# Weight splits, first chunk and last squares at the borders of three MLPs

## What is computed

```
def first_block(x, ...):
    h = x
    for layer in range(2):
        if layer == 0:
            h = h + gla_mixer(rms_norm(h, a_norm), ...)
        else:
            k_sh, v_sh = shared_kv(h, kv_norm, w_kv, k_norm)
            h = h + diff_mixer(rms_norm(h, b_norm), k_sh, v_sh, ...)
        h = h + sqrelu_mlp(rms_norm(h, mlp_norm[layer]), mlp_w1[layer], mlp_w2[layer])
    return h

def second_block(x, mem, ...):
    u = rms_norm_2(h, norm_mix)
    proj = u @ w_in
    ...
    h = h + merged @ w_mix_out
    h = h + memory_cross_attention(...)
    u = rms_norm_2(h, norm_mlp)
    h = h + jnp.square(jax.nn.relu(u @ w_mlp_up)) @ w_mlp_down
    return h
```

## Time and profile before

| | us |
|---|---|
| median of 3 runs | 1561.04 |
| fastest, slowest | 1559.62, 1563.72 |
| the profiled execution | 1560.55 |
| its span | 1558.6 |
| PE busy | 1421.5 (91%) |
| DVE busy | 1034.0 (66%) |
| ACT busy | 894.4 (57%) |
| POOL busy | 334.9 (21%) |

### The profile page before, as it was taken

One profiled execution on the slowest core, in us unless ns is written; L12 is line 12 of the kernel. 1 busy time (PEld: TensorE's weight loads), 2 busy tenths in 40 slices (PEclk: granted clock), 3 DMA queues, 4 the chain that ended last, 5 costly groups with the idle time before them and its releaser, 6 DMA issues. The chain is left out here.

```text
span 1558.6 us, 29975 instructions
## 1 busy us (share of the span) xinstructions
PE 1421.5 (91%) x11466; PEld 1289.0 (83%) x11466; DVE 1034.0 (66%) x1638; ACT 894.4 (57%) x1705; POOL 334.9 (21%) x337
## 2 busy tenths in 40 slices
PE   7998999999889999999887799898898889799999
PEld 6888899988668999989776677778777679599998
DVE  6787666566656666667999755567576666375555
ACT  4455555456556555558988645454565466365543
POOL 2002211150004111138877000004000003051111
PEclk9999999999978999999999899999999989999999
DMA  7323455545713555535344322325334335055552
GB/s 306 126 106 122 147 200 194 189 163 118 207 55 121 204 190 188 193 132 189 136 144 153 108 86 105 108 102 180 122 129 156 126 124 180 32 193 199 193 189 82
DMA packets 35603, 233.72 MB, mean 150 GB/s; under 512 B 4000, under 2 KB 7072, under 8 KB 8352
## 3 DMA queue, kind: packets, MB, share of 16 engines
q1 hardware_dynamic: 31104, 223.75, 40.4%
q10 hardware_dynamic: 3216, 4.19, 1.7%
q0 software_dynamic: 1168, 4.20, 0.9%
HBM read 227.93 MB, written 4.19 MB: 149 GB/s over the span
## 5 line engine op out<-in xcount | busy, mean ns | idle before, releaser
L1593 DVE TENSOR_TENSOR w_lo<-raw,w_hi 128x1024 bf16<-128x1024 f32 x420 | 535.6, 1276 | 230.2 <-ACT w_hi L997 226.8
L997 ACT CAST w_hi<-raw 128x1024 fp32r<-128x1024 f32 x420 | 438.4, 1047 | 329.1 <-PE ps L422 163.6
L412 PE MATMUL ps<-xa_both,w_hi 128*128 128x256 f32 x1808 | 467.9, 298 | 29.3 <-ACT w_hi L997 10.4
L413 PE MATMUL ps<-xa_both,w_hi 128*128 128x256 f32 x1808 | 441.1, 284 | 0.0
L412 PEld LDWEIGHTS ps<-xa_both,w_hi 128*128 128x128 f32 x1808 | 351.8, 195 | 42.6 <-issue 15.3
L413 PEld LDWEIGHTS ps<-xa_both,w_hi 128*128 128x128 f32 x1808 | 352.5, 195 | 0.9 <-issue 0.2
L422 PE MATMUL ps<-xa_bf,w_lo 128*128 128x256 bf16 x1808 | 240.7, 277 | 21.6 <-DVE w_lo L1593 21.6
L456 PE MATMUL ps<-xb_both,w_hi 128*128 128x256 f32 x832 | 204.7, 288 | 0.0
L422 PEld LDWEIGHTS ps<-xa_bf,w_lo 128*128 128x128 bf16 x1808 | 161.0, 99 | 49.5 <-DVE w_lo L1593 25.0
L457 PE MATMUL ps<-xb_both,w_hi 128*128 128x256 f32 x832 | 195.2, 277 | 0.0
L456 PEld LDWEIGHTS ps<-xb_both,w_hi 128*128 128x128 f32 x832 | 156.6, 188 | 1.5 <-DVE xb_both L1608 0.3
(11 more groups left out here) (297 smaller groups left out, 1868.4 us busy)
## 6 DMA issues: line engine op xcount, KB each, us to landing
raw<-weights SPq DMA_DIRECT2D x210, 1024.0 KB, 4.8
band<-arena ACTq DMA_DIRECT2D x1, 3072.0 KB, 35.5
arena<-band POOLq DMA_DIRECT2D x8, 256.0 KB, 3.2
arena<-gla_masks SPq DMA_DIRECT2D x1, 1088.0 KB, 15.0
H<-x_t SPq DMA_DIRECT2D x2, 512.0 KB, 4.4
arena<-mem_t POOLq DMA_DIRECT2D x1, 1024.0 KB, 5.3
arena<-band POOLq DMA_DIRECT2D x8, 128.0 KB, 2.9
out_t<-H ACTq DMA_DIRECT2D x8, 128.0 KB, 2.0
```

The lines of the kernel that those rows point to most:

```text
L412: mm(ps[:, bank, 0:T], w_hi[:, s, k], X.hi[:, k], start=k == 0, stop=False)
L413: mm(ps[:, bank, 0:T], w_hi[:, s, k], X.lo[:, k], start=False, stop=False)
L997: nc.scalar.copy(w_hi[:, j % HI_SLOTS].rearrange("p k n -> p (k n)"), raw[:, j // 2 % RING, j % 2]).then_inc(hi_done, 1)
L1593: TT(w_lo[:, j % HI_SLOTS].rearrange("p k n -> p (k n)"), raw[:, j // 2 % RING, j % 2], w_hi[:, j % HI_SLOTS].rearrange("p k n -> p (k n)" ...
```

## The change

At the borders where pairs arrive (gated linear attention to MLP 0, MLP 0 to the shared K, MLP 1 to the mixing layer), DVE now makes the splits of the next stage's second and third chunk behind the last pair. Rests 2 stand ahead of sum 3. POOL squares only rows 0 to 5 (11 steps), and DVE squares rows 6 and 7 together (`last_squares`), adds the two, waits for POOL's eleventh step, and adds the result to `sumsq`; its semaphore then counts the four steps that POOL leaves out. POOL waits once more, for the last pair's sum, before its `XB.bf`.

The first chunk of each MLP, of the shared K and of the mixing layer goes through `opening_chunk`: the products of rows 0 to 5, their six corrections, the products of rows 6 and 7, their two corrections. It waits for its own PSUM bank only. In MLP 0 the sums move from behind the first to behind the second chunk (on PE and ACT); in the mixing layer they move behind the `dt` matmuls.

```diff
+POOL_SQUARES = 2 * (KC - 2) - 1
...
+            def opening_chunk(c, j, X, build, evicted):
+                s, bank, late = j % HI_SLOTS, j % BANKS, (6, 7)
+                to = ps[:, bank, 0:T]
+                def products(ks):
+                    for k in ks:
+                        pe.wait_ge(X.lo_done, KC * build + k + 1)
+                        mm(to, w_hi[:, s, k], X.hi[:, k], start=k == 0, stop=False)
+                        mm(to, w_hi[:, s, k], X.lo[:, k], start=False, stop=False)
+                def rests(ks):
+                    for k in ks:
+                        pe.wait_ge(X.bf_done, KC * build + k + 1)
+                        last = mm(to, w_lo[:, s, k], X.bf[:, k], start=False, stop=k == KC - 1)
+                    return last
+                pe.wait_ge(hi_done, c + 1)
+                pe.wait_ge(bank_free, evicted)
+                products(range(6))
+                pe.wait_ge(lo_done, c + 1)
+                rests(range(6))
+                products(late)
+                rests(late).then_inc(gemm_done, 1)
...
-            mlp(C_M0, 0, XA_MLP0, XB_MLP0, 1)
+            mlp(C_M0, 0, XA_MLP0, C_GO + 2, 1, XB_MLP0, 1)
...
-                if n < 8:
-                    chunk(C_DK + n, n, XA, XA_DIFF if n == 0 else None)
+                if n == 0:
+                    opening_chunk(C_DK, 0, XA, XA_DIFF, C_DK - 8)
+                elif n < 8:
+                    chunk(C_DK + n, n, XA, None)
...
-            chunk(C_CONV, C_CONV, XA, XA_MIX)
+            opening_chunk(C_CONV, 0, XA, XA_MIX, C_CONV - 8)
             chunk(C_CONV + 1, C_CONV + 1, XA, None)
-            stats(4, True, True)
...
             last.then_inc(sa["dtf"], 1)
+            stats(4, True, True)
...
+            def last_squares(nu):
+                done(TT(hn_sqb[:], H[:, 6:8], H[:, 6:8], ALU.mult))
+                done(TT(hn_sqb[:, 0], hn_sqb[:, 0], hn_sqb[:, 1], ALU.add))
+                dve.wait_ge(sq_step, (2 * KC - 1) * nu + POOL_SQUARES)
+                TT(sumsq[:], sumsq[:], hn_sqb[:, 0], ALU.add).then_inc(sq_step, 2 * KC - 1 - POOL_SQUARES)
...
-                        cut_lo(c + 8 + j + AHEAD, o + j + AHEAD)
+                        if not last or X is None or j <= 5:
+                            cut_lo(c + 8 + j + AHEAD, o + j + AHEAD)
...
+                    if last and X is not None:
+                        pair_lo(2, X, build, gain)
                     if last:
                         pair_sum(3, c0 + 56, down_pair(3))
-                        if X is not None:
-                            pair_lo(2, X, build, gain)
-                            pair_lo(3, X, build, gain)
+                    if last and X is not None:
+                        pair_lo(3, X, build, gain)
+                        last_squares(nu + 1)
+                        for j in (6, 7):
+                            cut_lo(c + 8 + j + AHEAD, o + j + AHEAD)
...
-            for p in range(4):
+            for p in range(3):
                 pair_sum(p, C_GO, gate_pair(p))
-                if p < 3:
-                    cut_lo(C_M0 + p, C_M0 + p)
-                if p:
+                if p == 0:
+                    cut_lo(C_M0, C_M0)
+                else:
                     pair_lo(p - 1, XA, XA_MLP0, "mlp_norm0")
+            pair_lo(2, XA, XA_MLP0, "mlp_norm0")
+            pair_sum(3, C_GO, gate_pair(3))
             pair_lo(3, XA, XA_MLP0, "mlp_norm0")
+            last_squares(1)
+            for c in (C_M0 + 1, C_M0 + 2):
+                cut_lo(c, c)
...
-                sum_squares(nu, H, bank_free, lambda k: c0 + k // 2 * 2 + 2)
+                sum_squares(nu, H, bank_free, lambda k: c0 + k // 2 * 2 + 2, KC - 2)
+                steps[0] += 2 * KC - 1 - POOL_SQUARES
...
             pool.wait_ge(gemm_done, C_DK)
+            pool.wait_ge(bank_free, C_DK)
```

More of the change, by code:

```diff
@@ L488, in head_sums, with mlp @@
                 mm(head_sums_at(k), bones, hn_sqb[:, k % 2], start=True, stop=True).then_inc(hn_mm, 1)
-            def mlp(c0, m, x_build, xb_build0, nu):
+            def mlp(c0, m, x_build, x_evicted, stats_at, xb_build0, nu):
                 o = c0 % 8
@@ L496, in group @@
                     for j in range(8):
-                        chunk(c + j, o + j, XA, x_build if first and j == 0 else None)
                         if first and j == 0:
+                            opening_chunk(c, o, XA, x_build, x_evicted)
+                        else:
+                            chunk(c + j, o + j, XA, None)
+                        if first and j == stats_at:
                             stats(nu, True, False)
@@ L708, in _ @@
             chunks(C_DO, 8, XB, XB_DO)
-            mlp(C_M1, 1, XA_MLP1, XB_MLP1, 3)
-            chunk(C_CONV, C_CONV, XA, XA_MIX)
+            mlp(C_M1, 1, XA_MLP1, C_M1 - 3, 0, XB_MLP1, 3)
+            opening_chunk(C_CONV, 0, XA, XA_MIX, C_CONV - 8)
             chunk(C_CONV + 1, C_CONV + 1, XA, None)
-            stats(4, True, True)
             pe.wait_ge(split_hi, 2)
@@ L967, in _ @@
             chunks(C_XO, 8, XB, XB_XO)
-            mlp(C_M2, 2, XA_MLP2, XB_MLP2, 7)
+            mlp(C_M2, 2, XA_MLP2, C_M2 - 3, 0, XB_MLP2, 7)
         @block.scalar
@@ L1048, in pair_operands, with mlp @@
                     A(X.bf[:, n], H[:, n], ACT.Copy, scale=pcol(gain, n)).then_inc(X.bf_done, 1)
-            def mlp(c0, m, nu, X, build, gain):
+            def mlp(c0, m, nu, stats_at, X, build, gain):
                 o = c0 % 8
@@ L1060, in group @@
                         cut_hi(c + j + AHEAD, o + j + AHEAD)
-                        if first and j == 0:
+                        if first and j == stats_at:
                             rms(nu, rstd)
@@ L1183, in _ @@
                 pair_operands(p, C_GO, XA, XA_MLP0, "mlp_norm0")
-            mlp(C_M0, 0, 1, XA, XA_DIFF, "kv_norm")
+            mlp(C_M0, 0, 1, 1, XA, XA_DIFF, "kv_norm")
             cut_hi(C_DK + AHEAD, C_DK + AHEAD)
@@ L1268, in _ @@
             nc.scalar.copy(dt_hi.rearrange("p k h -> p (k h)"), pcol("w_dt", 0, KC * SSD_HEADS)).then_inc(split_hi, 1)
-            mlp(C_M1, 1, 3, XA, XA_MIX, "norm_mix")
+            mlp(C_M1, 1, 3, 0, XA, XA_MIX, "norm_mix")
             for n in range(2):
@@ L1567, in _ @@
             residual(C_XO, XA, XA_MLP2, "norm_mlp2")
-            mlp(C_M2, 2, 7, None, None, None)
+            mlp(C_M2, 2, 7, 0, None, None, None)
             for n in range(KC):
@@ L2199, in _, with sum_squares @@
             steps = [0]
-            def sum_squares(nu, src, ready, base):
-                for k in range(KC):
+            def sum_squares(nu, src, ready, base, n=KC):
+                for k in range(n):
                     pool.wait_ge(ready, base(k))
```

## The result

The changed kernel takes 1545.54 us (median of five runs, 1544.34 to 1547.8), the kernel before 1559.62 beside it (1555.47 to 1563.72): a ratio of 0.9907, 95% interval 0.9892 to 0.9921, or 14.1 us less.

What follows compares the result with a forecast made beforehand. DVE's queue ends last at the borders, PE's half clock being its echo. Gains of 5.0 + 2.4 + 3.7 + 0.6 = 11.7 us put the median at 1549.3 us, down from 1561.04; range 1545.5 to 1556.0.

Steps and rivals of the forecast that it cites:

- A: Border from gated linear attention's output to MLP 0: third chunk at 162.5 in place of 167.51, 5.0 us gained.
- C: Border from MLP 1 to the mixing layer: third chunk at 686.4 in place of 690.12, 3.7 us gained.
- the last two L1608 take 1.7: At A, DVE's last two rows of `lo` behind the last pair's sum: 1.7 us, ending at 158.5 against 159.48 before.
- POOL's eleventh step ends at 158.44: At A, POOL ends its squares before DVE's last squares begin, so these take 1.7 us, not 3.0.
- B: Border from MLP 0 to the shared K: DVE's queue ends last, 2.4 us gained, between 0.8 and 3.1.
- D and E: Borders into MLP 1 and into MLP 2: corrections lie over the wait for row 7, 0.3 us each, 0 to 0.5.
- shift as a whole: Stages behind the borders move with them, PE being their bound or the chain from rstd; no size given.
- Rival 1: PE's clock falls all the same: 1551.8 us at one border, 1555.5 at all three; chance 0.18 at two or three.
- Rival 2: DVE and POOL get into each other's way at A, B and C: gain 7.3 us, 1553.7; chance 0.17.
- Rival 3: Raw weights land late because splits free their slabs later: 1562 us or more; chance 0.02.
- Rival 4: PE is held somewhere else (second chunk, banks): gain only 3 to 4 us, 1557; chance 0.05.
- the chance of 0.06: More gained than forecast, to 15.5 us, with B at 3.1 and contention gone where POOL stops early.

Runs made afterwards that it cites:

- later head sums: Changed kernel with TensorE's sums over a key head one chunk later in the stage behind B: 1543.87 us, ratio 0.9894.
- repeat of the change: The changed kernel measured again with no edit, against the kernel before on the same chip: 1545.16 us, ratio 0.9905.
- splits and squares: Kernel before with moved splits and last squares on VectorE, without opening chunk and later sums: 1551.17 us, ratio 0.9942; measured again, 1549.43 us, ratio 0.9931.

## Why the prediction was right, and where it was not

**What bounds the kernel.** Right in the main. DVE's queue ended last at the borders, and the splits between the pairs were the larger part (9.1 of 15.1 us when taken out). That PE's half clock was the echo of that queue is not shown: at A and C the clock stayed up where the rows came earlier, but at A it also stayed at 1.00 with the squares moved alone and without the moved splits, where PE took its last row 5.2 and 5.9 us behind the start (before 5.6, in the changed kernel 3.4).

**A, 5.0 forecast, 6.35 measured.** The mechanism was right and the size too small. The mis-sized term is "the last two L1608 take 1.7" and, behind it, "POOL's eleventh step ends at 158.44". The prediction moved DVE's splits but left POOL's steps where the rows of before had them. Two of those steps were long only because a split ran beside them (1.54 and 1.76; now 0.61 and 0.90, and 1.52 and 1.77 again with the splits put back), so POOL was done 2.0 us sooner, and the last two rows ran with POOL all but done (154.40 against 154.51): 0.89, not 1.7. Four rows beside POOL took 2.99, not 3.4. Together DVE was through with its rows 3.2 us behind the start, not 4.5, and the third chunk came at 7.20, not 8.5. The squares were sized right: 155.20 to 156.78, 1.6 for 1.7. The new wait for the split was there, but about 0.25 us, not 0.55, as DVE came sooner.

**B, 2.4 forecast, 3.4 measured.** By the prediction's own mark, the first scaled eviction, it was 4.8. Behind the start of B it was to come at 12.0 and came at 9.56: 1.2 from DVE's rows as at A, 0.9 from the splits, taken at 1.49 and measured at 1.2, and 0.45 from the small instructions, whose 1.24 held a long L1790 (0.69, now L1838 0.15). Then the clock fell in the third chunk and took 1.4 back. The prediction treated B's gain as ended at the eviction; what stands late next, PE's 2.2 us for the first head's squares, was in the trace of before and not named. Why the clock fell there and not in three runs with the same wait stays open.

**C, 3.7 forecast, 4.98 measured.** The same 1.3 us as at A, by the same rows. The sums behind dt were hidden, as said: PE has no wait for what rstd releases. But 1.7 us are given back between C and E, where the prediction let the stages behind "shift as a whole".

**D and E.** 0.3 forecast for each, 0.30 and 0.30 measured.

**Rivals.** Rival 1 (the clock falls all the same) came true at B, later than it put it, and at neither of the others. Rival 2 named the right pair of engines and, at B, the wrong payer. Beside each other at B, the splits took 1.22 to 1.27 and POOL's eight steps 12.64 us in place of 7.45:

```profile
344.73 7.45 POOL L2267 TENSOR_SCALAR xb_bf<-H,par 128x256 bf16<-128x256 f32 x8
```

(the kernel before), and now

```profile
330.49 12.64 POOL L2317 TENSOR_SCALAR xb_bf<-H,par 128x256 bf16<-128x256 f32 x8
```

POOL had the time, so nothing waited. The Trainium skill (GPSIMD Engine Reference, Specifications) has the two share their SBUF interfaces; these rows agree, but by that rule alone B was to gain 0.8, and which side pays decided. The prediction took a split at 1.49 with 2.0 as a bound; a row of the kernel before at A that it didn't read, 1.73 beside POOL (shown below), says that DVE could have paid as well. Rival 3 (late raw weights) did not show: the page's raw transfers still land in 4.8 us, and ScalarE's casts (L1028) wait for no transfer at A, B or C. Rival 4 fell with the result.

**The sum.** The borders gave 15.3 us against 11.7; the medians 14.1 and 15.1, since other stages moved by 1 to 2 us either way. So the first result lies inside the range although the three large terms were all too small. The case that happened is nearly the one with the chance of 0.06, more gained than forecast because contention is gone where POOL stops early: its mechanism had been seen and counted as unlikely, though POOL's rows beside a split at A (1.54, 1.76) showed it.

## What to carry to other kernels

When an instruction is moved out of one engine's queue, replay the neighbour engine too: a step that was long because of what ran beside it gets short, and what waits behind it comes sooner; take its length from a row of the same form that stood alone. Where parts of a change unblock the same chunk, cost them as taken out of the whole and not one by one: by the medians the moved splits were worth 5.5 us alone and 9.1 with the squares and the sums out of their way, and the three parts alone (5.5, 2.7 and 1.9) fall 5 us short of the whole. And a stage's gain is not won until the next place where TensorE waits has been looked at, since a stretch at half clock that is saved at one place can turn up in another.

## What the runs showed of the hardware

- At the borders POOL mostly pays for DVE's two-input splits: its square of 128x256 takes 0.61 alone and 1.41 to 1.54 beside a split, its add 0.73 to 0.90 and 1.58 to 1.77, its scaled copy 0.93 and 1.58 in the mean of eight. The split takes 1.20 to 1.23 with POOL idle and 1.21 to 1.27 at the changed kernel's B, but it can pay too: 1.49, up to 2.13 in the mixing layer (726.89 in the kernel before, beside L2283), and 1.73 at A before, where POOL's step stood first:

```profile
159.42 1.73 DVE L1593 TENSOR_TENSOR w_lo<-raw,w_hi 128x1024 bf16<-128x1024 f32 x1
```

```profile
159.28 0.79 POOL L2215 TENSOR_TENSOR sumsq<-sumsq,sqtmp 128x256 f32<-128x256 f32 x1
```

With DVE's 128x256 rows of `lo` it is DVE that pays: 0.44 each with POOL idle, 0.75 to 0.86 beside it.
- A single wait doesn't tell the clock. With the splits moved alone, PE stood 1.16 and 2.42 us within the first chunks of A at 1.00 throughout; in the kernel before it fell there with no wait above 0.73, and with the squares moved alone it held through the same waits. One wait of 1.52 us for ScalarE, at 382.89 with the later head sums and at 384.42 in the repeat of the change, was followed by 0.57 in the one (384 to 388) and by 1.00 in the other (386 to 390), with the same instructions around it:

```profile
382.89 0.70 PE L699 MATMUL ps<-arena 64*128 64x256 f32 x4 [1.52 <-ACT arena L1271]
```

```profile
384.42 0.70 PE L699 MATMUL ps<-arena 64*128 64x256 f32 x4 [1.52 <-ACT arena L1271]
```

So the same code has the half-clock stretch in one program and not in another, and two executions of one program, on two chips, differed by 3.4 us between C and E (splits and squares). A difference of 1 to 3 us between two versions may be no more than that.
